# Loading expert weights in pairs of 1 MB units, 16 KB in a row per partition

## What is computed

```python
def swiglu(h, w_gate, w_up, w_down):
    return (jax.nn.silu(h @ w_gate) * (h @ w_up)) @ w_down
...
    def expert_block(args):
        xb, e = args
        return swiglu(xb, w_gate[e], w_up[e], w_down[e])
...
    contrib = out[dest] * gate_sorted[:, None].astype(out.dtype)
    y = jnp.zeros((T, D), h.dtype).at[tok_sorted].add(contrib)
```

## Time and profile before

| | us |
|---|---|
| median of 3 runs (1283.83 to 1284.49) | 1284.08 |
| the profiled execution | 1283.14 |
| its span, first to last instruction | 1281.1 |
| PE busy | 1263.7 (99%) |
| PE busy with weight loads | 740.7 (58%) |
| DVE, ACT, POOL busy | 635.4, 280.7, 89.0 |
| DMA queue of SP, share of 16 engines | 82.7% |

### The profile page before, as it was taken

One profiled execution on the slowest core, in us unless ns is written; L12 is line 12 of the kernel. 1 busy time (PEld: TensorE's weight loads), 2 busy tenths in 40 slices (PEclk: granted clock), 3 DMA queues, 4 the chain that ended last, 5 costly groups with the idle time before them and its releaser, 6 DMA issues.

```text
span 1281.1 us, 25001 instructions
## 1 busy us (share of the span) xinstructions
PE 1263.7 (99%) x10418; PEld 740.7 (58%) x10418; DVE 635.4 (50%) x1442; ACT 280.7 (22%) x426; POOL 89.0 (7%) x127
## 2 busy tenths in 40 slices
PE   9999999999999999999999999999999999999978
PEld 5778888888897444444444444444444444444423
DVE  5988565666788353333533423353353333335533
ACT  4864443333695100010010001001001000100101
POOL 3402111111001000000000000000000000000010
PEclk9999999999999999999999999999999999999999
DMA  8827555556359699999999999999999999999995
GB/s 306 273 108 279 206 196 196 196 196 187 125 214 407 253 399 411 425 412 424 425 413 410 426 412 405 425 419 405 423 425 406 405 424 413 413 425 426 424 426 245
DMA packets 87960, 442.29 MB, mean 345 GB/s; under 512 B 7362, under 2 KB 18452, under 8 KB 44596
## 3 DMA queue, kind: packets, MB, share of 16 engines
q1 hardware_dynamic: 83232, 424.96, 82.7%
q0 software_dynamic: 4560, 15.85, 3.5%
q10 hardware_dynamic: 68, 0.02, 0.0%
HBM read 430.84 MB, written 9.57 MB: 344 GB/s over the span
## 4 chain that ended last, share of the span: by engine, by line
PE 96%; DMA 2%; SPq 1%; DVE 0%; ACT 0%; issue 0%; DVEq 0%
PE psum L1822 63%; PE psum L469 9%; PE psum L471 9%; PE psum L470 9%; DMA raw_more<-in_moe_w_down 2%; PE psum L1327 1%; SPq L719 1%; PE psum L1828 1%; PE psum L1473 0%; PE psum L1482 0%; PE psum L1500 0%; PE psum L1313 0%; PE psum L1774 0%; PE psum L1457 0%; PE psum L1587 0%; PE psum L1472 0%
## 5 line engine op out<-in xcount | busy, mean ns | idle before, releaser
L1822 PE MATMUL psum<-raw_more,hT 128*32 128x512 f32 x1592 | 482.0, 592 | 4.8 <-DMA raw_more<-in_moe_w_down 4.8
L1822 PE MATMUL psum<-raw,hT 128*32 128x512 f32 x984 | 303.1, 592 | 0.6 <-DMA raw<-in_moe_w_down 0.4
L1822 PE MATMUL psum<-raw_more,xg 128*32 128x512 f32 x1704 | 241.8, 592 | 0.1
L1822 PE MATMUL psum<-raw_more,xg_odd 128*32 128x512 f32 x1536 | 217.8, 597 | 5.6 <-DMA raw_more<-in_moe_up_last 3.1
L1822 PEld LDWEIGHTS psum<-raw_more,hT 128*32 128x32 f32 x1592 | 133.0, 109 | 121.8 <-issue 117.1
L2729 DVE STREAM_TRANSPOSE hT<-hid 32x128 f32<-32x128 f32 x588 | 177.7, 302 | 9.0
L2719 DVE SCALAR_TENSOR_TENSOR hid<-hid,psum 96x512 f32<-96x512 f32 x48 | 32.8, 684 | 263.9 <-PE psum L1822 263.2
L1258 ACT ACTIVATE hid<-psum 96x1024 f32<-96x1024 f32 (+1 forms) x28 | 25.6, 913 | 575.0 <-PE psum L1822 410.0
L1822 PE MATMUL psum<-raw,xg 128*32 128x512 f32 x984 | 144.2, 592 | 0.0
L1822 PEld LDWEIGHTS psum<-raw_more,xg 128*32 128x32 f32 x1704 | 83.0, 110 | 84.1 <-issue 83.0
L1822 PE MATMUL psum<-raw,xg_odd 128*32 128x512 f32 x928 | 131.4, 592 | 0.0
(11 more groups left out here) (409 smaller groups left out, 1409.0 us busy)
## 6 DMA issues: line engine op xcount, KB each, us to landing
raw_more<-in_moe_w_down SPq DMA_DIRECT2D x69, 1024.0 KB, 15.2
raw_more<-in_moe_up_wide SPq DMA_DIRECT2D x61, 1024.0 KB, 14.1
raw_more<-in_moe_gate_wide SPq DMA_DIRECT2D x60, 1024.0 KB, 13.7
raw<-in_moe_w_down SPq DMA_DIRECT2D x43, 1024.0 KB, 15.0
raw<-in_moe_gate_wide SPq DMA_DIRECT2D x36, 1024.0 KB, 14.5
raw<-in_moe_up_wide SPq DMA_DIRECT2D x35, 1024.0 KB, 13.8
raw<-in_ffn_w_gate SPq DMA_DIRECT2D x14, 1024.0 KB, 5.1
raw<-in_ffn_w_up SPq DMA_DIRECT2D x14, 1024.0 KB, 5.8
```

What stands on the lines that cost most here:

```text
L1822: return pe.matmul(psum[rows_q, bank, cols], stationary, moving, start=start, stop=stop, tile_position=(0, rows_q.start), skip_group_check ...
```

## The change

Two units that belong together (q = 0 and 1, or 2 and 3, or the two halves of a down step) now stand next to each other in `LOADS`, at the place of the earlier first use. `RING_PLACES` is reordered so that places 2k and 2k + 1 lie side by side in a tile in six of eight cases. Where they do, both units are loaded by one DMA of 2 MB, 16 KB in a row per partition, after both places have been left; its landing is told by the even place's semaphore. The other two pairs of places (4, 5 and 6, 7), the first 16 loads and the last two are loaded one unit at a time, each after its own place has been left, from half of a 16 KB row. The host lays all three weights out in pairs. PE waits for the pair's semaphore in `arrived`; the rest of PE's program is as it was.

```diff
-        RING_PLACES = [(3, 1), (3, 2), (5, 1), (5, 2), (4, 1), (4, 2), (0, 1), (0, 2),
+        RING_PLACES = [(3, 1), (4, 1), (4, 2), (5, 2), (5, 1), (0, 2), (0, 1), (3, 2),
+                       (0, 0), (1, 0), (2, 0), (3, 0), (4, 0), (5, 0), (1, 2), (2, 2)]
+        PLACES_LEFT = [(3, 1), (3, 2), (5, 1), (5, 2), (4, 1), (4, 2), (0, 1), (0, 2),
                        (1, 0), (2, 0), (5, 0), (0, 0), (3, 0), (4, 0), (1, 2), (2, 2)]
...
+        def pair_of(u):
+            m, w, q = u
+            return (m, w, q // 2)
+
+        def units_of(pair):
+            m, w, q = pair
+            return [(m, w, 2 * q), (m, w, 2 * q + 1)]
+
+        PAIRS = sorted((min(first_use(e, u) for u in units_of(pair)), e, pair[0] is None, pair[1:], pair[0] or 0)
+                       for e in range(E) for pair in {pair_of(u) for u in FIRST_USE})
+        LOADS = [(e, u) for at, e, is_down, rest, m in PAIRS for u in units_of((None if is_down else m,) + rest)]
...
+        def side_by_side(n):
+
+            (s, part), (s_next, part_next) = RING_PLACES[n], RING_PLACES[n + 1]
+            return s_next == s + 1 and part_next == part
+
+        def alone(i):
+
+            return not side_by_side(i % RING // 2 * 2) or i >= len(LOADS) - 2
+
+        ODD_ALONE = [sum(alone(i) for i in range(RING + n, len(LOADS), RING)) for n in range(RING)]
+
+        def pair_ring(n):
+            s, part = RING_PLACES[n]
+            t, at = (raw, s) if part == 0 else (raw_more, s + (part - 1) * SLOTS)
+            return t[:, at:at + 2].rearrange("p a b -> p (a b)")
...
+            def pass_loads(p):
+
+                expert_of = {0: 0}
+                if isinstance(p, int):
+                    assert all(e == 0 for e, u in LOADS[:RING])
+                    first_loads()
+                for i in range(RING if isinstance(p, int) else 0, len(LOADS), 2):
+                    e, u = LOADS[i]
+                    if e not in expert_of:
+                        if len(expert_of) == 1:
+                            sp.wait_ge(plan_ready, 2)
+                        expert_of[e] = sp.value_load(slot_expert[0:1, e:e + 1], min_val=1, max_val=E - 1)
                     e = expert_of[e]
-                    if m is None:
-                        src = moe_down[e, w, q]
-                    elif WIDTH[m] == 2:
-                        src = moe_wide[w][e, m, q]
+                    n = i % RING
+                    left = [gone(*LOADS[i - RING + k]) - (E * UNITS if i < RING else 0) for k in range(2)]
+                    if alone(i) and (i >= RING or not side_by_side(n)):
+                        for k in range(2):
+                            sp.wait_ge(freed, p * (E * UNITS) + left[k])
+                            load_alone(e, LOADS[i + k][1], n + k)
                     else:
-                        src = moe_last[w][e, q]
-                    sp.dma_start(ring(n), src).then_inc(m_landed[n], 16)
+                        sp.wait_ge(freed, p * (E * UNITS) + max(left))
+                        sp.dma_start(pair_ring(n), rows_of(e, u)).then_inc(m_landed[n], 16)
...
             def arrived(p, e, u):
-                n = PLACE[e, u] % RING
-                pe.wait_ge(m_landed[n], p * (16 * LAPS) + 16 * (PLACE[e, u] // RING + 1 + before_ring(n)))
+
+                i = PLACE[e, u]
+                n, lap = i % RING, i // RING
+                if n % 2 == 0 or not side_by_side(n - 1):
+                    pe.wait_ge(m_landed[n], p * (16 * LAPS) + 16 * (lap + 1 + before_ring(n)))
+                    return
+                if not alone(i):
+                    pe.wait_ge(m_landed[n - 1], p * (16 * LAPS) + 16 * (lap + 1 + before_ring(n - 1)))
+                if lap == 0:
+                    pe.wait_ge(m_landed[n], 16 * (1 + before_ring(n)))
+                elif alone(i):
+                    pe.wait_ge(m_landed[n], p * (16 * ODD_ALONE[n]) + 16 * (2 + before_ring(n)))
...
+def pair_rows(units):
+
+    return units.swapaxes(-3, -2).reshape(units.shape[:-3] + (P, 2 * units.shape[-1]))
+
+
+def gate_rows(w):
 
     experts, d, f = w.shape
     wide = f // (2 * BANK) * 2 * BANK
-    first = w[:, :, :wide].reshape(experts, d // (2 * P), 2, P, wide // (2 * BANK), 2 * BANK)
-    last = w[:, :, wide:].reshape(experts, d // (4 * P), 4, P, BANK)
-    return (first.transpose(0, 4, 1, 3, 2, 5).reshape(experts, wide // (2 * BANK), d // (2 * P), P, 4 * BANK),
-            last.transpose(0, 1, 3, 2, 4).reshape(experts, d // (4 * P), P, 4 * BANK))
+    first = w[:, :, :wide].reshape(experts, d // (4 * P), 2, 2, P, wide // (2 * BANK), 2 * BANK)
+    first = first.transpose(0, 5, 1, 2, 4, 3, 6).reshape(experts, wide // (2 * BANK), d // (4 * P), 2, P, 4 * BANK)
+    last = w[:, :, wide:].reshape(experts, d // (4 * P), 4, P, BANK).transpose(0, 1, 3, 2, 4)
+    return pair_rows(first), pair_rows(last.reshape(experts, d // (4 * P), P, 4 * BANK))
+
+
+def down_rows(w):
+
+    experts, f, d = w.shape
+    return pair_rows(w.reshape(experts, f // BANK, 2, P, 2 * d))
```

More of the change, by code:

```diff
@@ L24, in trunk @@
           lru_w_x, lru_b_x, lru_lam, lru_w_out, ffn_w_gate, ffn_w_up, ffn_w_down, moe_w_router,
-          moe_gate_wide, moe_gate_last, moe_up_wide, moe_up_last, moe_w_down, out):
+          moe_gate_wide, moe_gate_last, moe_up_wide, moe_up_last, moe_down, out):
     T, D = x.shape[1], x.shape[2]
@@ L406, in trunk @@
         moe_wide, moe_last = (moe_gate_wide, moe_up_wide), (moe_gate_last, moe_up_last)
-        moe_down = moe_w_down[0].rearrange("e (j h p r) d -> e j h p (r d)", h=2, r=2, p=P)
         def unit(t, s, b):
@@ L575, in first_use @@
             return light_first[e, u] if (e, u) in light_first else ROUNDS * e + FIRST_USE[u]
-        LOADS = sorted((first_use(e, u), e, u[0] is None, u[1:], u[0] or 0)
-                       for e in range(E) for u in FIRST_USE)
-        LOADS = [(e, (None if is_down else m,) + rest) for at, e, is_down, rest, m in LOADS]
+        def pair_of(u):
[7 more added lines that the diff above has]
+        LOADS = [(e, u) for at, e, is_down, rest, m in PAIRS for u in units_of((None if is_down else m,) + rest)]
         PLACE = {load_: n for n, load_ in enumerate(LOADS)}
@@ L686, in _, with rows_of, load_alone, first_loads @@
                              lru_w_x[0].rearrange("h i j -> i h j")).then_inc(wx_landed, 16)
-            def pass_loads(p):
-                expert_of = {0: 0}
-                for i, (e, u) in enumerate(LOADS):
-                    if e not in expert_of:
-                        if len(expert_of) == 1:
-                            sp.wait_ge(plan_ready, 2)
-                        expert_of[e] = sp.value_load(slot_expert[0:1, e:e + 1], min_val=1, max_val=E - 1)
-                    n = i % RING
-                    s, part = RING_PLACES[n]
-                    if i >= RING:
-                        sp.wait_ge(freed, p * (E * UNITS) + gone(*LOADS[i - RING]))
-                    elif not isinstance(p, int):
-                        sp.wait_ge(freed, p * (E * UNITS) + (gone(*LOADS[i - RING]) - E * UNITS))
-                    elif (s, part) in ((1, 2), (2, 2)):
+            def rows_of(e, u):
+                m, w, q = u
+                if m is None:
+                    return moe_down[e, w]
+                return moe_wide[w][e, m, q // 2] if WIDTH[m] == 2 else moe_last[w][e]
+            def load_alone(e, u, n):
+                half = slice(u[2] % 2 * UNIT, (u[2] % 2 + 1) * UNIT)
+                sp.dma_start(ring(n), rows_of(e, u)[:, half]).then_inc(m_landed[n], 16)
+            def first_loads():
+                for s, part in PLACES_LEFT:
+                    n = RING_PLACES.index((s, part))
+                    if (s, part) in ((1, 2), (2, 2)):
                         sp.wait_ge(out_ps, 2 * TT)
@@ L2926 @@
         "lru_w_x", "lru_b_x", "lru_lam", "lru_w_out", "ffn_w_gate", "ffn_w_up", "ffn_w_down", "moe_w_router",
[L2927 to L2930 removed]
+        "moe_gate_wide", "moe_gate_last", "moe_up_wide", "moe_up_last", "moe_down"]
+def pair_rows(units):
+    return units.swapaxes(-3, -2).reshape(units.shape[:-3] + (P, 2 * units.shape[-1]))
+def gate_rows(w):
     experts, d, f = w.shape
     wide = f // (2 * BANK) * 2 * BANK
[L2934 to L2937 removed]
+    first = w[:, :, :wide].reshape(experts, d // (4 * P), 2, 2, P, wide // (2 * BANK), 2 * BANK)
[5 more added lines that the diff above has]
+    return pair_rows(w.reshape(experts, f // BANK, 2, P, 2 * d))
 def kernel(**inputs):
@@ L2949 @@
     for w in ("gate", "up"):
-        laid[f"moe_{w}_wide"], laid[f"moe_{w}_last"] = unit_rows(_np.asarray(inputs[f"moe_w_{w}"])[0])
+        laid[f"moe_{w}_wide"], laid[f"moe_{w}_last"] = gate_rows(_np.asarray(inputs[f"moe_w_{w}"])[0])
+    laid["moe_down"] = down_rows(_np.asarray(inputs["moe_w_down"])[0])
     for name in _INS:
```

4 lines of the change are left out of this document (1 added, 3 removed).

## The result

The changed kernel took 1294.82 us (median of 4 runs, 1293.78 to 1295.12), the kernel before 1283.95 in the same comparison: a ratio of 1.0085, with a 95% interval of 1.0072 to 1.0098, so 10.9 us more. A second set of runs of the same two kernels gave 1.0084 (1.0071 to 1.0098). The forecast was 1292.3 us, 0.65%: the sign and the mechanism held, 2.5 us are missing.

A forecast was written before the change was run, and what follows sets the result against it. PE paces experts 0 to 6 with DMA just keeping up; DMA paces the light last expert. Late landings +6.9, rate gain −1.0 and grain at the end +2.4 give +8.3 us on 1284.08: 1292.3 us, own range 1289 to 1295.

The forecast's parts named there:

- the sign: Whole kernel: slower by 0.65%, +8.3 us; slower had a chance of 0.86, same 0.08, faster 0.06.
- the mechanism: Load queue near 1085 us: pairs wait for both places, the queue runs dry, landings 6.9 us late; coarse end adds 2.4.

The follow-up runs named there:

- The kernel with 37 pairs: Kernel before, its load order kept, with the changed kernel's ring layout and 16 KB rows, and 2 MB pairs only where nothing waits for them: 1283.49 us, 0.9999.
- units one by one: Changed kernel with its order of loads and layout kept, but every unit loaded and waited for by itself: 1291.30 us, 1.0055 to the kernel before.
- two loads behind each wait: Changed kernel with its waits for both places kept, but two 1 MB loads, each with its own landing, instead of one 2 MB load: 1293.57 us, 1.0067.
- the down pairs later: Changed kernel with down pairs sorted by their second unit's first use: 1284.29 us with the last eight units loaded alone, 1286.38 us with the end as changed.

## What to carry over

When a full queue paces a kernel, time in which it runs dry is lost for the most part even when it is early, and whole when it is late, and one late wait is enough; look for the moment at which the least work is queued, and count what stands in the list ahead of the wait. When small loads are merged, a merged load whose second place is left late should not stand at the head of the list: here sorting the down pairs by the later of their two first uses, not by the earlier, took away 7.9 of 10.9 us. Then keep the last few loads small, since PE can start on nothing of a merged one until all of it is there. If merging isn't slower after that, ask what it was to gain: here the queue moved 425 GB/s before and 428 after.

## What was not expected of the hardware

The other queue's small transfers take longer beside the 2 MB loads. DMA issues of the kernel before (KB each, median us to landing), beside the earlier trace rows:

```profile
y_rows<-y_sum POOLq DMA_DIRECT2D x7, 384.0 KB, 8.1
```

The changed kernel:

```profile
raw_more<-x_rows POOLq DMA_DIRECT2D x7, 384.0 KB, 14.9
y_rows<-y_sum POOLq DMA_DIRECT2D x7, 384.0 KB, 10.1
```

The kernel with 37 pairs:

```profile
raw_more<-x_rows POOLq DMA_DIRECT2D x7, 384.0 KB, 11.3
```

With 119 pairs the 384 KB of rows of 4 KB take 14.9 us instead of 11.3 and 10.1 instead of 8.1. With units one by one the first was 11.4, with two loads behind each wait 11.5, with the down pairs later 15.1. So it comes with the 2 MB loads in rows of 16 KB and not with the late issue; whether the size of the load or the length of the row does it, no run separates. In the kernel with 37 pairs it doesn't show, but there hardly a pair is under way beside these rows: of their seven loads two meet none, and five start 1 to 3 us before a pair lands. It cost nothing here, since PE waited for none of these rows.
